# Two transformer blocks on one core: features-first copies of x and of the memory, and all value products placed first

## What is computed

```python
def rmsnorm(x, g):
    r = lax.rsqrt(jnp.mean(x * x, axis=-1, keepdims=True) + EPS)
    return x * r * g

h = rmsnorm(x, mix_pre_g)                      # 256 x 1024
proj = h @ w_in                                # 1024 -> u, v_s, q, k, v_a, g_a, g_b, f_logit
...
kv = mem @ wkv                                 # mem: 256 x 1024, keys and values of cross-attention
```

## Time and profile before

| | us |
|---|---|
| median of 3 runs | 1488.92 |
| lowest, highest | 1487.26, 1491.27 |
| profiled execution, whole time | 1489.12 |
| its span (first to last instruction) | 1487.4 |
| TensorE busy in the span | 1149.6 (77%) |
| VectorE, ScalarE, GpSimd busy | 464.2, 401.3, 73.6 |
| mean DMA rate over the span | 338 GB/s |

### The profile page before, as it was taken

The page is one execution under the profiler, slowest core; times in us unless marked ns, Lnnn a source line. Parts: engine busy times, 40 slices in busy tenths (PEclk is TensorE's granted clock), DMA queues, the critical chain, the costliest instruction groups (busy, mean ns, idle before and its releaser), DMA issues.

```text
span 1487.4 us, 19365 instructions
## 1 busy us (share of the span) xinstructions
PE 1149.6 (77%) x8332; PEld 755.1 (51%) x8332; DVE 464.2 (31%) x939; ACT 401.3 (27%) x898; POOL 73.6 (5%) x89
## 2 busy tenths in 40 slices
PE   9999999999998997996566556566565665565677
PEld 7888988888877875442222223223222232232234
DVE  6575777656788754010000000000000000000002
ACT  5665567555666643100000000000000000000002
POOL 0000020000035311000000000000000000000000
PEclk9999999999999998798778788787877787887799
DMA  8445546555553487999999999999999999999996
GB/s 314 170 140 200 199 170 229 210 198 199 198 186 114 157 350 306 406 434 441 427 434 436 427 433 433 434 433 438 420 446 424 427 441 425 434 431 438 424 423 286
DMA packets 29305, 503.32 MB, mean 338 GB/s; under 512 B 4130, under 2 KB 4770, under 8 KB 8100
## 3 DMA queue, kind: packets, MB, share of 16 engines
q1 hardware_dynamic: 25344, 493.43, 79.8%
q10 hardware_dynamic: 3876, 8.65, 1.6%
HBM read 501.02 MB, written 1.05 MB: 338 GB/s over the span
## 4 chain that ended last, share of the span: by engine, by line
issue 60%; PE 32%; DVE 5%; ACT 2%; POOL 1%; POOLq 0%; DVEq 0%; ACTq 0%
PE PB L374 9%; PE PB L354 5%; PE PB L355 5%; PE PB L356 5%; PE PB L375 4%; DVE SPL L1575 1%; DVE XN L1595 0%; PE PB L405 0%; POOL SP L2213 0%; PE PB L811 0%; PE PB L676 0%; PE PB L414 0%; PE PB L503 0%; ACT SPH L1041 0%; PE PB L795 0%
## 5 line engine op out<-in xcount | busy, mean ns | idle before, releaser
L913 PE MATMUL PB<-RING,XS 128*32 128x512 f32 x2048 | 294.1, 722 | 175.8 <-DMA RING<-in_wgu_dram 175.4
L913 PEld LDWEIGHTS PB<-RING,XS 128*32 128x32 f32 x2048 | 67.1, 126 | 345.5 <-issue 250.1
L945 PE MATMUL PB<-RING,HHT 128*32 128x256 f32 x2048 | 149.9, 450 | 110.5 <-DMA RING<-in_wdn_dram 109.1
L1575 DVE TENSOR_TENSOR SPL<-RAW,SPH 128x512 fp32r<-128x512 f32 x318 | 206.9, 708 | 31.3 <-ACT SPH L1041 28.7
L374 PE MATMUL PB<-XT,SPH 128*128 128x512 f32 x544 | 194.1, 401 | 0.0
L1041 ACT ACTIVATE SPH<-RAW 128x512 fp32r<-128x512 f32 x340 | 186.8, 620 | 7.2 <-DMA RAW<-in_wst_dram 3.1
L945 PEld LDWEIGHTS PB<-RING,HHT 128*32 128x32 f32 x2048 | 75.4, 128 | 169.7 <-issue 138.8
L375 PE MATMUL PB<-XT,SPL 128*128 128x256 f32 x544 | 152.3, 280 | 0.0
L1509 ACT ACTIVATE SG<-PB 128x512 f32<-128x512 f32 x16 | 9.6, 597 | 505.5 <-PE PB L913 505.5
L2103 DVE SCALAR_TENSOR_TENSOR YL<-PB,COLS,YH 128x256 fp32r<-128x256 f32 x64 | 31.0, 484 | 276.7 <-ACT YH L1523 276.7
L374 PEld LDWEIGHTS PB<-XT,SPH 128*128 128x128 f32 x544 | 102.2, 188 | 24.6
(11 more groups left out here) (393 smaller groups left out, 1575.6 us busy)
## 6 DMA issues: line engine op xcount, KB each, us to landing
RAW<-in_wst_dram SPq DMA_DIRECT2D x84, 1024.0 KB, 4.8
RING<-in_wgu_dram SPq DMA_DIRECT2D x13, 2048.0 KB, 40.2
RING<-in_wgu_dram SPq DMA_DIRECT2D x4, 4096.0 KB, 21.8
RING<-in_wgu_dram SPq DMA_DIRECT2D x14, 1024.0 KB, 8.2
RING<-in_wdn_dram SPq DMA_DIRECT2D x6, 2048.0 KB, 13.5
RING<-in_wdn_dram SPq DMA_DIRECT2D x2, 4096.0 KB, 17.9
RING<-in_wdn_dram SPq DMA_DIRECT2D x3, 1024.0 KB, 41.2
RAW<-in_wst_dram SPq DMA_DIRECT2D x4, 256.0 KB, 5.6
```

What stands on the lines that cost most here:

```text
L913: i = e.matmul(PB[b][32 * c:32 * c + 32, :], XS[x % 2][:, k, :], chunk_at(n)[:, 512 * c:512 * c + 512], start=k == 0, stop=k == KD - 1)
L945: w = e.matmul(PB[b][32 * j:32 * j + 32, 0:T], HHT[:, j, 32 * c:32 * c + 32], chunk_at(n)[:, T * (4 * (c % 2) + j):T * (4 * (c % 2) + j + ...
L1575: e.tensor_tensor(l, src, h.bitcast(F32), ALU.subtract).then_inc(*lo.up())
```

## The change

The host also lays out x with the features first (`xt`, 1 MB more to load) and the memory features first (`mem`, the same size as before), and gives the gain as 128 x 8 columns (`GCOL`). In the kernel:

- x times gain is split straight from `xt`, without the norm factor: sixteen ScalarE copies of 128 x 128 with the gain column as scale (`XRH`), sixteen VectorE instructions for the low part (`XRL`).
- All values come first: 48 products of the first half, then 48 of the second half, from the unscaled rows; units 2 and 3 now hold the second half of the value weights, and the units of queries and keys follow. The factor of each token is applied in `values_out`, which moves to after the setup loads, with eight weight pieces between its two halves.
- Between the two halves, two small products on TensorE spread the factors along the columns into PSUM bank 6; VectorE scales `XR` by them in place (eight instructions of 128 x 256), ScalarE and VectorE split that into `XT` (two instructions of 128 x 1024 each).
- Gone are the transposes of x and of the memory and the products that spread the gain row.

Some of the diff:

```diff
-U_VA, U_Q, U_K = (0, 6), (2, 8), (4, 10)
+U_VA, U_Q, U_K = (0, 2), (4, 8), (6, 10)
...
+        for half_ in range(2):
+            for j in range(2):
+                for t in range(2):
+                    for k in range(4):
+                        if half_ == 0:
+                            e.wait_ge(*vec.at(("xr", t, 4 * j + k)))
+                        i = rk(U_VA[half_] + j, k, 4 * j + k, 2 - 2 * half_ + t, XRH, XRL, t, j + k == 0, j == 1 and k == 3)
...
+            if half_ == 0:
+                e.wait_ge(s_id, 16)
+                for t in range(2):
+                    e.wait_ge(*gps.at(("r", f"x{t}")))
+                    i = e.matmul(PB[6][:, tiles[t]], rn[f"x{t}"].to_broadcast([P, P]), ident, start=True, stop=True)
+                i.then_inc(*mixd.up("r_in"))
+        free = {b: act.at(("va", int(b < 2), b % 2)) for b in range(4)}
...
-        e.wait_ge(s_mem, 16)
-        for t in range(2):
-            for j in range(2):
-                b = 2 * t + j
-                e.wait_ge(*free[b])
-                for k in range(4 * j, 4 * j + 4):
-                    i = e.transpose(PB[b][:, (k % 4) * P:(k % 4 + 1) * P], MEM[:, t, k * P:(k + 1) * P], ident)
-                i.then_inc(*turn.up(("mem", t, j)))
...
+        e.dma_start(GCOL[:, :], io["mix_pre_g"]).then_inc(s_gcol, 16)
+        e.dma_start(XR[:, 1, 0:4, :], io["xt"][:, 1, 0:4, :]).then_inc(s_xt[1], 16)
+        e.dma_start(CON[:, 0:128], io["con"][:, 0:128]).then_inc(s_id, 16)
+        for t in range(2):
+            e.dma_start(XR[:, t, 4:8, :], io["xt"][:, t, 4:8, :]).then_inc(s_xt[2 + t], 16)
...
+        high_rows(0, 0)
+        high(4)
+        high_rows(1, 0)
+        high_rows(0, 1)
+        high(2)
+        high_rows(1, 1)
         squares_in(0, 0, "x0", (s_x[0], 16))
-        high(2)
+        squares_in(1, 0, "x1", (s_x[1], 16))
+        high(6)
         for j in range(2):
-            high_turned(0, j, j, XTH, turn.at(("in", 0, j)), "xt_in")
...
+            e.wait_ge(*vec.at(("n_in", 4 * j + 3)))
+            e.activation(XTH[:, 4 * j:4 * j + 4, :].rearrange("p k (t c) -> p k t c", t=2),
+                         XR[:, :, 4 * j:4 * j + 4, :].rearrange("p t k c -> p k t c"), ACT.Copy).then_inc(*act.up(("xt_in", j)))
         high(4)
...
+        for t in range(2):
+            e.wait_ge(*gps.at(("r", f"x{t}")))
+        for t in range(2):
+            values_out(0, t)
+        high(8)
+        for t in range(2):
+            values_out(1, t)
```

More of the change, by code:

```diff
@@ L409, in tensor @@
         e.wait_ge(*gps.at("warm"))
-        for _ in range(7):
+        for _ in range(10):
             e.matmul(PB[4][:, 0:P], WARM[:, :], WARM[:, :], start=True, stop=True)
[L412 to L426, removed]
+        for half_ in range(2):
[5 more added lines that the diff above has]
+                        i = rk(U_VA[half_] + j, k, 4 * j + k, 2 - 2 * half_ + t, XRH, XRL, t, j + k == 0, j == 1 and k == 3)
+                    if j or t:
+                        i.then_inc(*prod.up(*([("va", half_, t)] if j else []), *([("unit", U_VA[half_] + j)] if t else [])))
+            if half_ == 0:
[5 more added lines that the diff above has]
+        free = {b: act.at(("va", int(b < 2), b % 2)) for b in range(4)}
+        for j in range(2):
+            e.wait_ge(*vec.at(("xt_in", j)))
         def fox_scores(h):
@@ L493, in tensor @@
                 e.wait_ge(*free[bank])
-                rtile(U_VS + 2 * h, bank, t, [("xt_in", t, j) for j in range(2)], ("vs", h, t))
+                rtile(U_VS + 2 * h, bank, t, [("xt_in", j) for j in range(2)], ("vs", h, t))
                 free[bank] = act.at(("vs", t, h))
@@ L544, in tensor @@
         out_tile(1)
-        turn_tile(XN, 0, (0, 1), [vec.at(("n_ffn", 0, j)) for j in range(2)], [vec.at(("memt", 0, j)) for j in range(2)], "ffn")
-        free = {2: vec.at(("memt", 1, 0)), 3: vec.at(("memt", 1, 1))}
-        e.wait_ge(*vec.at(("memt", 1, 1)))
+        turn_tile(XN, 0, (0, 1), [vec.at(("n_ffn", 0, j)) for j in range(2)], [free[j] for j in range(2)], "ffn")
+        e.wait_ge(*vec.at(("memt", 3)))
         for b in range(4):
@@ L1198, in scalar @@
         e.wait_ge(*vec.at(("gu", 7)))
-        for t in range(2):
-            for j in range(2):
-                high_turned(t, j, 2 * t + j, MEMH, turn.at(("mem", t, j)), "memt")
+        e.wait_ge(s_mem, 16)
+        for q in range(4):
+            e.activation(MEMH[:, 2 * q:2 * q + 2, :], MEM[:, 2 * q:2 * q + 2, :], ACT.Copy).then_inc(*act.up(("memt", q)))
         post_squares(0, "po0", "out")
@@ L1618, in vector, with low_rows @@
[L1618 to L1621, removed]
-        low(2)
-        for j in range(2):
[L1624 to L1628, removed]
+        def low_rows(t, j):
+            if t + j == 0:
+                e.wait_ge(s_gcol, 16)
+            for k in range(4 * j, 4 * j + 4):
+                e.wait_ge(*act.at(("xr", t, k)))
+                e.scalar_tensor_tensor(out=XRL[:, k, tiles[t]], in0=XR[:, t, k, :], scalar=GCOL[:, k:k + 1], in1=XRH[:, k, tiles[t]].bitcast(F32),
+                                       op0=ALU.mult, op1=ALU.subtract).then_inc(*vec.up(("xr", t, k)))
@@ new lines, in vector @@
+        low_rows(0, 0)
+        low(4)
+        low_rows(1, 0)
+        low_rows(0, 1)
+        low(2)
+        low_rows(1, 1)
+        low(2)
+        for t in range(2):
+            e.wait_ge(s_x[t], 16)
+            e.tensor_tensor_reduce(XN[:, t, halves[1]], X[:, t, halves[1]], X[:, t, halves[1]], 1.0 / D, 0.0, ALU.mult, ALU.add, ss[f"x{t}"][1]).then_inc(*vec.up())
+        for t in range(2):
+            mean_square(f"x{t}", act.at((f"x{t}", 0)), vec.so_far())
+        low(4)
+        e.wait_ge(*mixd.at("r_in"))
@@ L1629, in vector @@
+        for j in range(2):
+            for k in range(4 * j, 4 * j + 4):
+                e.scalar_tensor_tensor(out=XR[:, :, k, :], in0=XR[:, :, k, :], scalar=GCOL[:, k:k + 1],
+                                       in1=PB[6][:, 0:T].rearrange("p (t c) -> p t c", t=2), op0=ALU.mult, op1=ALU.mult).then_inc(*vec.up(("n_in", k)))
         for j in range(2):
-            low_turned(1, j, j, XTH, XTL, "xt_in")
-        low(8)
+            e.wait_ge(*act.at(("xt_in", j)))
+            e.tensor_tensor(XTL[:, 4 * j:4 * j + 4, :].rearrange("p k (t c) -> p k t c", t=2), XR[:, :, 4 * j:4 * j + 4, :].rearrange("p t k c -> p k t c"),
+                            XTH[:, 4 * j:4 * j + 4, :].rearrange("p k (t c) -> p k t c", t=2).bitcast(F32), ALU.subtract).then_inc(*vec.up(("xt_in", j)))
@@ L1634, in joined @@
+        low(12)
         def joined(dst, bank, name, scale=1.0):
@@ L2257, in sync @@
             e.dma_start(RAW[0][:, c], io["wst"][0][:, c]).then_inc(s_first[q], 16)
-        e.dma_start(X[:, 1, :], io["x"][P:T, :]).then_inc(s_x[2], 16)
+        for t in range(2):
+            e.dma_start(X[:, t, :], io["x"][t * P:(t + 1) * P, :]).then_inc(s_x[t], 16)
         def unit_split(u):
@@ L2489, in lay_out @@
         "x": a["x"][0],
-        "mem": a["mem_2"][0],
+        "xt": np.ascontiguousarray(a["x"][0].reshape(2, P, 8, P).transpose(3, 0, 2, 1)),
+        "mem": np.ascontiguousarray(a["mem_2"][0].reshape(T, 8, P).transpose(2, 1, 0)),
         "norm_mix_g_2": a["norm_mix_g_2"][0],
```

65 lines of the change are left out of this document (25 added, 40 removed).

## The result

| | before | changed |
|---|---|---|
| median, us | 1488.92 | 1495.55 |
| lowest, highest of 5 runs | 1487.26, 1491.27 | 1493.59, 1497.14 |
| profiled execution, its span | 1489.12, 1487.4 | 1497.14, 1495.4 |

The changed kernel is slower: the ratio is 1.0041, 95% interval 1.0029 to 1.0053. Its profiled execution is the slowest of its five runs, 1.6 us above their median.

What follows compares the result with a forecast made beforehand. TensorE was taken to bound the kernel until 414 us. The mark's +5.4 and the memory's -0.3 summed to +5.1 to 5.2 us on 1488.9, giving 1494.1 us; range 1490.2 to 1498.2.

Steps and rivals of the forecast that it cites:

- The bound and the mark: TensorE sets the pace to 414 us; mark (96 value products, four query blocks done) moves from 47.5 by +5.4 us.
- First product: The first value product on TensorE can start near 7.8 us instead of 11.53.
- Unit 1: Weight unit 1's load, behind xt's added megabyte, lands at 14.7 us; bounds 13.3 and 16.0, or 16.9 by the skill's rule.
- The norm on VectorE: VectorE scales XR in eight instructions of 128 x 256, 0.35 us each in a run, done at 28.5.
- The added wait: Query block 0 waits for ScalarE's eviction of bank 0 until 39.9 us; TensorE idles 3.3 us.
- The clock: Two idle stretches of TensorE, at unit 1 and before query block 0, cost 1.7 us each; bounds 0 and 1.7.
- The memory: Its transposes (1.92 us) go, but out_tile(0) waits for GpSimd's pieces: -0.3 us, bounds -1.9 and +1.4.
- As meant: ScalarE and VectorE keep TensorE fed, bank 0 free in time: mark 43.1, -4.4; total 1484.2 us; chance 0.05.
- Dearer: Unit 1 at 16 or 16.9, or gain column late; clock stretch lost at memory: +8 to +11, 1498.3 us; chance 0.13.
- Cheap: Wait there, but unit 1 at 13.3, one or both clock losses out: +0.4 to +3.2, 1490.7 us; chance 0.20.

Runs made afterwards that it cites:

- the loads on SP: Changed kernel with only the nine setup loads moved from ScalarE's program to SP's, behind unit 3's issue: ratio 1.0028.
- The mended order: Changed kernel with xt's second halves, x, setup loads, squares, unit 3's split, bank 0/1 evictions reordered, two unit 30 pieces on VectorE: ratio 0.9980, 1486.23 us.

## Why the prediction held, step by step

**The bound and the mark: right.** TensorE's loss before 55 us is found again, within 0.2 us, at 72, at 414 and at the end. That it is found so closely at the end is partly luck: in the ten other profiles the shift against before changes by -0.4 to +4.6 us between 414 us and the end, with the clock's falls near 480 us among the reasons.

**First product.** It came at 9.29, not at 7.8: the first quarter of unit 0 landed at 7.8 instead of 6.5, behind the other transfers. Nothing hung on it, since unit 1 was late anyway.

**Unit 1: the term that was mis-sized.** I took 14.7 between 13.3 and 16.0; it was 16.8, above the upper bound. Every later step is late by as much or a little more: the low part of piece 7 some 2.1 us (22.2 against 20.05), the factor products done 2.4 (28.1 against 25.65), query block 0 2.6 (42.5 against 39.9), the mark 2.5 (55.4 against 52.9). What failed is the price of a megabyte, made from two windows that both lie in the first 7 us, where the rate was not steady. The rule of the Trainium skill's page "DMA: Bandwidth & Descriptors" (section "Issuing engines are not separate DMA queues"), that transfers of all issuing engines share the same DMA engines, agrees with these runs: later than 8 us the rate was 408 with two queues and 444 with one. Its estimate in the prediction, 16.9, hit the landing, though the 295 GB/s from which it was worked out are not a queue's rate.

**The norm on VectorE.** 3.22 us for eight, 0.40 each instead of the estimated 0.35:

```profile
28.14 3.22 DVE L1645 SCALAR_TENSOR_TENSOR XR<-XR,GCOL,PB 128x256 f32<-128x256 f32 x8 [1.77 <-PE PB L431]
```

**The added wait: right in mechanism, a little smaller.** The nine issues stood where they were expected, took 4.74 us (4.86 forecast), and ScalarE's pieces of unit 3 ran beside them. TensorE idled for 2.37 us, not 3.3: query block 0 came 2.6 us later than forecast, but the last value product was over 3.5 us later (40.15 against 36.6). The delay of unit 1 and the slower norm are in both, up to the end of the norm (31.36 against 28.5). Behind it the products lost another 0.6 us: from 34.37 on TensorE had all 24 products of unit 3 to do and was itself the limit, where I had fifteen behind the last low part. Bank 0 got some 0.3 back: the issues began at 31.41, while the second copy into `XT` still ran. Both experiments that shorten the queue ahead of bank 0 took some 2 us off (2.5 and 1.9 by the ratios).

**The clock: one of the bounds, not a fixed cost.** I added 1.7 us twice. The profiled execution has both falls, another has one, a third none. With unit 1 at its 16.8 (2.1 us later) and the norm at its 3.22 (0.4 more), my +5.4 at the mark becomes 7.9 with both falls, 6.2 with one and 4.5 with none; the three executions stand at 8.0, 6.4 and 5.0, and the medians 6.6 apart in the first session and 8.5 in the later one. So the nearness of 1494.1 to 1495.55 owes something to luck: two terms were 2.5 us too small, and the falls, counted twice, come in some executions only.

**The memory: right.** -0.2 us (7.98 to 7.80) for -0.3 forecast, with GpSimd's pieces as the reason; two idle times of 0.52 and 0.72 us for 0.8 each, and no fall of the clock there:

```profile
208.05 0.50 PE L358 MATMUL PB<-SPH,MTL 128*128 128x512 f32 x1 [0.52 <-POOL SPL L2187]
...
209.74 0.50 PE L358 MATMUL PB<-SPH,MTL 128*128 128x512 f32 x1 [0.72 <-POOL SPL L2187]
```

**The rivals.** "As meant" needed bank 0 free and weights in time. The mended order gives it just that and passes the mark 2.8 us ahead, where the rival had 4.4 (the 3.1 of its median hold the two pieces moved to VectorE as well): a start without transposes can pay, but the change left the queues as they fell. "Dearer" had unit 1 at 16 or 16.9 as a condition, and that came true (16.8); its other two did not: the gain column landed at 0.81 + 3.3 = 4.1 us, and no clock was lost at the memory. "Cheap" had unit 1 at 13.3, which didn't come. Its sum was wrong as well: 5.1 less 1.4 and less one or two falls is +0.3 to +2.0, not +0.4 to +3.2.

## What to carry over

A scheme that frees one engine's start is worth what the in-order programs of its helpers let through: before moving work, list what stands ahead of each new wait on the same engine, DMA issues included, and move the wait or the queue with it. Price added bytes by a steady stretch of the transfer rate and add what the start takes, and put the loads in the order in which they are needed. Where an idle time sits next to a fall of the clock, look at a second execution before counting the fall.

## What was not expected of the hardware

The same 1.8 us of idle before 21.1 to 21.7 us were followed by a fall of the granted clock in two profiles (the changed kernel's first, and that with the loads on SP) and by none in three; after 2.4 to 2.7 us before query block 0 it fell in two of three. The Trainium skill's page "TensorE: Matmul & The Clock Gate" (section "Part 1: The HAM clock gate (the "warmup" mystery)") says that the monitor's windows run freely and don't start with the kernel; that would make falls depend on where an idle time lies in them. The two and three of five above agree with that; that the windows are the cause is not shown.

The DMA rate of the first microseconds is uneven: 127 GB/s from 4 to 6 us and 408 from 8 to 10 in the same program, with a DMA share of 0.85 and 1.06, so the engines counted as busy while they moved little. With the extra megabyte alone, 133 GB/s in the same window go with a share of 0.59.
